# Two residual blocks on one core: the position table's traffic, the first chunks and the residual of the feed-forward stages

## The reference

```python
def _swiglu(x, wg, wu, wd):
    return (jax.nn.silu(x @ wg) * (x @ wu)) @ wd

for l in range(DEPTH):                                    # DEPTH 2, D_FF 2816
    h = 0.5 * _swiglu(x, ffn_w_gate[l, 0], ffn_w_up[l, 0], ffn_w_down[l, 0])
    x = _layernorm(ALPHA * x + h, ln_g[l, 0], ln_b[l, 0])
    h = _mixer(x, ..., band_bias, valid)                  # band_bias from rel_bias
    x = _layernorm(ALPHA * x + h, ln_g[l, 1], ln_b[l, 1])
    h = 0.5 * _swiglu(x, ffn_w_gate[l, 1], ffn_w_up[l, 1], ffn_w_down[l, 1])
    x = _layernorm(ALPHA * x + h, ln_g[l, 2], ln_b[l, 2])
```

## Time and profile before

| | |
|---|---|
| median of 3 runs | 2622.07 us (2621.82 to 2624.2) |
| the profiled execution's own time | 2620.62 us |
| its span, from first to last instruction | 2618.8 us |
| TensorE busy | 2551.7 us, 97% of the span |
| VectorE busy | 1203.6 us, 46% |
| ScalarE busy | 503.8 us, 19% |
| TensorE's mean granted clock | 0.995 of 2.4 GHz |

### The profile page before, as it was taken

How to read it: one execution, slowest core, us unless ns; L and a number is a source line. 1 busy time by engine, 2 the same in 40 slices (tenths; PEclk the granted TensorE clock), 3 DMA queues, 4 the chain that set the end, 5 groups by cost and what they waited for, 6 DMA issues and landing times.

```text
span 2618.8 us, 41458 instructions
## 1 busy us (share of the span) xinstructions
PE 2551.7 (97%) x17331; PEld 1630.4 (62%) x17331; DVE 1203.6 (46%) x2527; ACT 503.8 (19%) x1041; POOL 11.0 (0%) x23
## 2 busy tenths in 40 slices
PE   7899999999999999999999999999999999999998
PEld 6775888668748887587788888533333343333332
DVE  4564766556656575535567664322212222221223
ACT  1111321011113311215422224211111111111111
POOL 0100000000000000000000000000000000000000
PEclk9999999999999999999999999999999999999999
DMA  7545244454454444552300104899999999999997
GB/s 262 179 177 209 97 193 161 167 202 165 173 181 173 160 162 161 211 207 81 113 19 4 51 4 180 327 420 420 420 420 414 420 420 413 420 420 416 407 420 294
DMA packets 92079, 637.75 MB, mean 244 GB/s; under 512 B 10680, under 2 KB 10680, under 8 KB 18576
## 3 DMA queue, kind: packets, MB, share of 16 engines
q1 hardware_dynamic: 90288, 629.67, 60.5%
q0 software_dynamic: 1600, 5.38, 1.0%
HBM read 632.38 MB, written 2.62 MB: 242 GB/s over the span
## 4 chain that ended last, share of the span: by engine, by line
PE 93%; DMA 3%; DVE 2%; ACT 1%; issue 1%; SPq 0%; DVEq 0%
PE ps L1449 27%; PE ps L726 18%; PE ps L794 10%; PE ps L983 6%; PE ps L874 4%; DMA ring<-weights 3%; PE ps L1407 3%; PE ps L934 2%; PE ps L1387 2%; PE ps L717 2%; PE ps L1232 2%; PE ps L1243 1%; PE ps L1248 1%; PE ps L1030 1%; PE ps L1347 1%; PE ps L1438 1%
## 5 line engine op out<-in xcount | busy, mean ns | idle before, releaser
L1449 PE MATMUL ps<-ring,arena 128*64 128x512 f32 (+1 forms) x1248 | 338.2, 593 | 1.5 <-ACT arena L1957 0.7
L1449 PE MATMUL ps<-arena 128*64 128x512 f32 (+1 forms) x1224 | 337.3, 593 | 1.0 <-ACT arena L1957 0.7
L1449 PEld LDWEIGHTS ps<-ring,arena 128*64 128x64 f32 (+1 forms) x1248 | 110.8, 141 | 182.7 <-issue 174.9
L726 PE MATMUL ps<-arena 128*128 128x256 f32 x960 | 224.3, 382 | 0.0
L1449 PEld LDWEIGHTS ps<-arena 128*64 128x64 f32 (+1 forms) x1224 | 111.2, 142 | 174.7 <-issue 168.2
L2766 DVE TENSOR_SCALAR X<-ps 128x256 f32<-128x256 f32 (+1 forms) x64 | 28.8, 449 | 396.9 <-PE ps L1449 396.9
L726 PEld LDWEIGHTS ps<-arena 128*128 128x128 f32 x960 | 180.3, 191 | 25.4 <-issue 0.4
L983 PE MATMUL ps<-arena,ring 128*128 128x256 f32 x784 | 173.0, 380 | 0.0
L794 PE MATMUL ps<-arena 128*128 128x512 f32 x352 | 165.4, 591 | 0.0
L983 PEld LDWEIGHTS ps<-arena,ring 128*128 128x128 f32 x784 | 147.7, 190 | 25.0 <-issue 5.6
L726 PE MATMUL ps<-ring,X 128*128 128x256 f32 x640 | 151.4, 379 | 0.0
(11 more groups left out here) (548 smaller groups left out, 3694.6 us busy)
## 6 DMA issues: line engine op xcount, KB each, us to landing
ring<-weights SPq DMA_DIRECT2D x366, 1024.0 KB, 8.0
arena<-weights SPq DMA_DIRECT2D x153, 1024.0 KB, 19.5
con<-weights SPq DMA_DIRECT2D x25, 1024.0 KB, 19.9
vec<-weights SPq DMA_DIRECT2D x25, 1024.0 KB, 20.1
vec<-weights SPq DMA_DIRECT2D x25, 512.0 KB, 14.7
con<-weights SPq DMA_DIRECT2D x25, 512.0 KB, 17.3
con<-consts SPq DMA_DIRECT2D x1, 1872.5 KB, 16.6
vec<-vectors SPq DMA_DIRECT2D x1, 1671.5 KB, 20.1
```

The lines of the kernel that those rows point to most:

```text
L726: last = mm(ps[:, bank[q], 0:T], left[:, k, :], right[:, :, k, :], start=(k == 0), stop=(k == 3))
L1449: last = mm(put(half), stationary(4 * kq + k), part[:, at:at + 512], start=False, stop=(kq == 1 and k == 3))
```

## The change

In stage 0 four steps are placed elsewhere. GpSimd waits for 22 released blocks, that is for the end of the gate and up products, before it writes the table. In chunk 1 VectorE does `hidden(0, 1)` and `first_column(1)` ahead of `sums13(2)`. The decay constants are computed in chunk 5 instead of chunk 2. Only one scaled identity is made.

In all four stages the residual's 16 products with the scaled identity become transposes against the plain identity (TensorE's transpose mode, which passes the values through). The sum is therefore kept at 1/(2 ALPHA) of its former scale: the gated product carries a factor of 0.5/ALPHA in a three-operand instruction, and the epsilon of the layer norm is divided by ALPHA squared. The mixer's residual keeps `RES[:, 1, :]`.

```diff
@@ -651,6 +651,7 @@
             pool.wait_ge(dve_step, DVE_STEP["rv_ready"])
+            pool.wait_ge(block_used, FFN_AT[0] + 2 * FCH)
             pool.dma_start(rel_scratch, RV[0:HEADS, :].unsqueeze(1).broadcast_to([HEADS, P, 384])).then_inc(rv_stored, 16)
@@ -811,7 +812,7 @@
                     for k in range(4):
-                        mm(ps[:, M_BANK[which], k * P:(k + 1) * P], cols[:, k, :], RES[:, 0, :], start=(k == 0), stop=False, skip_group_check=True)
+                        mm(ps[:, M_BANK[which], k * P:(k + 1) * P], cols[:, k, :], ident, start=(k == 0), stop=False, is_transpose=True, skip_group_check=True)
@@ -2030,9 +2031,7 @@
                 dve.wait_ge(con_loaded, 16)
-                for which in range(2):
-                    last = v.tensor_scalar(RES[:, which, :], ident, (2.0 * ALPHA, ALPHA)[which], None, ALU.mult)
-                last.then_inc(dve_step, 1)
+                v.tensor_scalar(RES[:, 1, :], ident, ALPHA, None, ALU.mult).then_inc(dve_step, 1)
@@ -2073,7 +2072,7 @@
-                    v.tensor_tensor(HTK[h], up, SIL[h], ALU.mult).then_inc(hid_ready, 1)
+                    v.scalar_tensor_tensor(out=HTK[h], in0=up, scalar=0.5 / ALPHA, in1=SIL[h], op0=ALU.mult, op1=ALU.mult).then_inc(hid_ready, 1)
@@ -2140,11 +2139,17 @@
-                        at = sums13(j + 1, lambda: hidden(j - 1, 1))
+                        if j == 1 and n == 0:
+                            hidden(0, 1)
+                            first_column(1)
+                            at = sums13(2)
+                        else:
+                            at = sums13(j + 1, lambda: hidden(j - 1, 1))
                     else:
                         weight_sums(0)
                         hidden(j - 1, 1)
-                    first_column(j)
+                    if j > 1 or n:
+                        first_column(j)
@@ -2153,7 +2158,7 @@
-                    if j == 2 and n == 0:
+                    if j == 5 and n == 0:
                         decay_and_bias()
@@ -2826,7 +2831,7 @@
-            v.memset(EPS2[:, 3:4], 4.0 * LN_EPS).then_inc(pads_zeroed, 1)
+            v.memset(EPS2[:, 3:4], LN_EPS / ALPHA ** 2).then_inc(pads_zeroed, 1)
```

## The result

The changed kernel takes 2598.2 us (median of four runs, 2594.1 to 2599.8), the kernel before 2622.0; the ratio is 0.990, with a 95% interval from 0.989 to 0.992. Its profiled execution took 2599.02 us with a span of 2597.2, against 2620.62 and 2618.8. The median fell where the forecast put it, 23.8 us lower. The traces say how much of that closeness is due to the terms and how much is luck.

What follows compares the result with a forecast made beforehand. TensorE, busy 97% of the span, was taken as the bound, so only its waits or work could be won: 3.8 + 15.3 + 4.8 = 23.9 us, from a span of 2618.8 and time of 2620.62 to 2596.7, median 2598.2; range 2594 to 2612.

Steps and rivals of the forecast that it cites:

- Long hole and the clock behind it: Stage 0, chunk 3: without the table's write beside its loads, 15.3 us gained, including 11.84 of waiting and 2.5 of slower clock.
- First hole: Stage 0, chunk 1: TensorE's 3.21 us wait before the turn goes by VectorE's new order; 3.8 us gained by chunk 3.
- the new hole: Stage 0, before chunk 2's turn of `hidden(1, 0)`: a wait of 1.3 us takes the place of the 3.21.
- the 1.5 that I had set as a sign of being wrong: TensorE's first stage: no hole over 1.5 us expected in the profile after, one of about 1.3 near 38.
- such a fall only as a risk of the new hole: Chunk 2: a clock fall behind the new 1.3 us wait would cost up to 2.5 us more; not counted.
- Decay series: 21 small VectorE operations, 5.2 us, moved from chunk 2 to chunk 5: nought taken, bounds 0 and 0.6.
- Three-operand gated product: The 88 gated products: at most 0.06 us more each, hidden save in chunk 1 and perhaps 5; 0.1 us in all.
- Transposes: Residual in four stages: sixteen transposes take 1.76 instead of 3.57 us, 0.6 waited; 1.2 us per stage, 4.8 in all.
- Rivals 2 and 3: Residual: 2, transposes no cheaper, 2603, chance 0.07; 3, clock falls behind them, 10 us back, 2608, chance 0.04.
- Table beside the down products: Stage 0 downs: loads beside the moved write land in time, slack 3.4 and 2.1 us for downs 4 and 5; cost nought.
- Rivals 1 and 4: Down 4's loads starve: 1, until the write ends, 2611, chance 0.10; 4, until table reads end too, 2629, chance 0.04.
- The sum: Whole kernel: 3.8 + 15.3 + 4.8 = 23.9 us gained, median forecast 2598.2 us.

## Why the prediction was right, point by point

- **Long hole and the clock behind it, 15.3 us.** Right to the tenth: chunk 3 took 12.54 us. The write alone moved showed 14.5, and most of the missing 0.8 is the decay series' hole of 0.63. The loads for chunk 4 went out at 35.3 and 35.6 and landed in 4.8 and 6.9 us (forecast: about 35, by 44).
- **First hole, 3.8 us.** The mechanism was right: the turn in chunk 1 came at 29.16 (forecast 29.17) and chunk 2 began at 36.79 (36.7). But the lead at chunk 3 is 2.8, and the new hole is 2.06 us, beyond the 1.5 that I had set as a sign of being wrong. The step that failed is the sentence that the loads for `sums13(2)` still land at 30.9. In the ten profiled executions VectorE started on them between 30.66 and 32.10, and both orders follow that. In the old order the hole was 3.21 us (start at 30.94), 4.67 (31.79), 4.92 (31.94) and 5.34 (32.10). In the new one, with `sums24(2)` still ahead of `middle(1)`, it was 0.65 (30.70), 0.69 (30.73), 2.35 (32.05) and 2.06 (32.10). Like beside like, the order is worth 4.2 us at chunk 3 with an early landing (54.38 in the kernel before, 50.23 in the kernel with the write ahead of the loads) and 4.4 with a late one (55.99 in the kernel with the decay series moved, 51.60 in the changed kernel). So the forecast 3.8 was near; it is the comparison of one early with one late execution that shows 2.8. What moves the landing by 1.4 us from one execution to the next stays open.
- **What the 3.8 contained without my saying so.** Behind the old hole TensorE also lost 1.5 us at the lower clock: its next eight records took 3.2 us from start to start instead of 1.73, and the granted clock was 0.50 from 33.2 to 36.6. I named such a fall only as a risk of the new hole; behind its 2.06 us there was none (the next eight records start at 41.01 and the ones behind them at 42.74).

```profile
32.83 3.25 PE L726 MATMUL ps<-arena 128*128 128x256 f32 x8
...
33.20:36.60 3.40, 3.40 (x11) 1.90 (x9) 3.37 (x6) 1.90 (x5) 0.00 (x0) 0.50 0.45 188
```

- **Decay series, nought.** Right; the estimated margin of 0.1 us held.
- **Three-operand gated product.** The bound of 0.06 us was not used up: it takes 0.42 us in the trace, as the two-operand one. The taps' 482 ns read their factor from memory, this one has it as a constant. That this makes the difference wasn't tried.
- **Transposes, 4.8 us.** Right: 1.17 us in stage 0, and 4.7 in four by the trace of the changed kernel (19.3 to 22.8 in three stages, and 1.2 before), with a wait of 0.43 us where I had 0.6, the way to TensorE included. Rivals 2 and 3, no cheaper transposes and a falling clock, are excluded by the kernel with the transposes alone.
- **Table beside the down products, nought.** Right, with a reserve larger than I worked out: I put the first pair's landings at 23.2 and 30.2, measured 4.7 and 7.6. Even without the start they were 15.1 and 22.0. Rivals 1 and 4 are excluded by these landings: the blocks of downs 4 to 6 were there at 155.1, 158.3 and 183.3, and the write landed at 188.6. What decides is where the write stands against the distance from issue to need: 18 to 19 us for a pair in the gate and up phase, about 28 for a block in the down phase (my estimate from the earlier trace rows: issue at 160.7, wanted 1.9 us ahead of down 6 at 190.8), with landings of 22 to 30 beside one write in the first and up to 22.6 in the second. Doubled traffic, with 42 and 49 for downs 6 and 7, went over it and cost 22 us.
- **The sum.** The terms give 23.9, the trace 22.8 at the end of the four stages and 21.6 at the end, the medians 23.8. The 1.1 us between the first two is the 1.2 by which the loads of the profiled execution landed later. That the median hit the forecast to a tenth is chance all the same: the four runs of the changed kernel spread over 5.8 us, the opening loads move an execution by up to 2 us, and the recurrence's clock by some us more. What sets that clock's short falls from run to run stays open; no kernel here tried to change it.

## What to carry to other kernels

When a slow transfer shares the queues with prefetched loads, work out for each phase the time from a load's issue to its need, and put the transfer where that is longer than the landings beside it; and issue it with or just behind a load rather than ahead of one. A hole that ends with a load's landing is not a constant: read it in several executions, compare executions whose loads landed alike, and prefer an order of the waiting engine in which it doesn't matter. Values that only pass through TensorE cost half as transposes (here 0.11 instead of 0.22 us for a 128x128 float32 tile), if the scale can be carried elsewhere.

## What the runs showed of the hardware that I had not expected

- Two writes of the same kind, issued 1.2 us apart, went side by side: they landed 65 and 78 us after their issue, against 37 for one, and the weight loads beside them took 34 to 49 us instead of 11 to 23. The slowing follows the amount of such traffic in flight, not only its presence.
- Two loads issued 0.7 and 0.3 us ahead of such a write landed in 4.7 and 7.6 us, two issued 1.0 and 1.4 us behind it in 15.1 and 22.0.
- SyncE's issue of a load, mostly 0.33 or 0.43 us, can itself get long beside one such write: 4.55 us for the load issued at 40.7 in the kernel before, which landed last and set the long hole. Beside the write at the down steps of the changed kernel, where single loads go out 6 us apart, it stayed at 0.33. With both writes in flight it took up to 6.9 us, so that the queue itself became late:

```profile
L595 SPq DMA_DIRECT2D ring<-weights x1: 6892/6892/6892, 178.9 to 178.9; - x1
```
